# Two transformer blocks on one core: in the even layer, weight loads go ahead of the gate tile, and ScalarE moves two products ahead of two roots

## The chip, the cores and the metric

One core of one Trainium2 chip runs the whole program in one launch. The metric is the device time of one execution in microseconds, lower is better. Engines are named as in the profile: PE is TensorE's matmul, PEld its weight load, DVE is VectorE, ACT is ScalarE, POOL is GpSimd, SP is SyncE, which issues the DMAs.

## The reference, cut to what matters

The program is a chain of layers on a 512 x 1024 float32 activation: an even layer (gated linear recurrence and short convolution), an odd layer (gated linear attention), then a second block with feed-forward and attention layers. Only the even layer is touched:

```python
h = rmsnorm(x, norm_pre)
proj = h @ w_in                      # 1024 -> 6 x 1024
xa, za, xb, gb, gc, zb = split(proj)
ua = centred_dwconv(xa, conv_w, 2) + conv_b
r, i = sigmoid(gates(ua))            # per head 128 x 128, two directions
a = exp(-8 r softplus(-lam)); b = sqrt(-expm1(2 log a)) * (i * ua)
h_f, h_b = scan forward, scan backward
ya = (h_f + h_b) * silu(za)
yb = gb * centred_dwconv(gc * xb, sc_w, 1) * silu(zb)
y = concat(ya, yb) @ w_out
```

## The kernel before, in words

**Tiling.** The activation lies transposed: features on the 128 partitions, 512 tokens along the free axis, so one matrix of 1024 x 128 weights ("slot") gives one tile of 128 x 512 outputs. Every float32 product is made of three fp32r products, `hi*hi`, `hi*lo` and `lo*hi`: `product` (lines 357 to 368) issues 3 x 8 = 24 matmuls per slot (lines 364, 365, 366).

**The even layer** goes through eight channels (heads) 0 to 7. A channel has six slots, numbered n = 0 to 5 within it and s = 0 to 47 over the layer: xa, xb, gc, gb, zb (silu), za (silu). On PE `even_channel` (line 668) runs the six products of a channel into four PSUM banks (s % 4) and then `even_gates` (line 658): eight matmuls (line 664) that multiply the channel's `ua` by the four gate matrices. Channel 0 is special: it works on the input before its norm is known. In channel 1 the gates of channel 0 are put behind its first product; from channel 2 on the order is six products, then the gates of the same channel.

**Weights.** SP loads each slot's 512 KB into a ring of four places (`even_weight`, DMA at line 591). A place may be written when POOL has split the slot before it (semaphore `w_ready`). POOL (`split_slot`, lines 321 to 335) casts a slot to `w_hi` (line 332) and subtracts to get `w_lo` (line 334). These two have two places each, so a slot's split waits until PE has finished the product two slots before (`slots_used`).

**The gate tile.** `gw` has two places (jj = channel % 2). One DMA of 264 KB (`gate_weight`, line 594) brings the gate matrices, their biases and the convolutions' weights of a channel. It may be written when the channel two before is entirely done. That is what SP waits for (`even_channel_done`, line 615), ahead of the gate tile and of all six slots of the channel.

**The order on ACT** (`even_act`, line 1314). Per channel: six moves of products out of PSUM (line 1325; the last two are Silu), four sigmoids of the gates (lines 1337, 1338), two Exp and two Tanh (lines 1346, 1348), and two square roots (line 1355), each of which waits for DVE. The moves free PSUM banks: product s + 4 waits for move s (`even_moved`).

**The order on DVE** (`even_dve`, line 1739). Per channel: the convolution of xa (lines 1774, 1777), which ends in `ua_ready`, for which the gates on PE wait; the convolution of xb (1801 to 1811); then, once ACT has the decays, squares and factors (1817 to 1821), two times product and scan (1825, 1828), the sum (1830) and the product with silu(za) (1832), which signals `even_channel_done`. DVE takes the channels strictly one after the other, so `ua` of a channel stands behind all of the channel before.

After channel 7 PE goes on with the layer's output product (`even_out`, lines 712 to 714), and the rest of the program follows.

Of the kernel before, what the change touches and what calls it, by code (L numbers as in the profile page):

```python
# [10 lines left out]
ACT = mybir.ActivationFunctionType  # L11
# [5 lines left out]
T = 512  # L17
# [13 lines left out]
RING = 4  # L31
# [73 lines left out]
def build(nc, x_in, consts_in, gates_in, weights, out):  # L105
    ctx = ExitStack()
    with ctx:
        sem = {}
# [46 lines left out]
        ps = ctx.enter_context(nc.psum_tensor("ps", [P, 8, 512], F32))  # L155
# [24 lines left out]
        for name, slots, cols in STREAM:  # L180
            first[name] = n0
            n0 += slots
        slots_of = {name: slots for name, slots, _ in STREAM}
        cols_of = {name: cols for name, _, cols in STREAM}

        def used(name, n):

            return n + (first[name] + 2)
# [229 lines left out]
        xa_pad, xb_s, gc_s, gb_s, szb, sza, ua = (r.tiles(2, n) for n in (516, T, T, T, T, T, T))  # L418
# [168 lines left out]
        @block.sync  # L587
        def _(sp):
            def even_weight(i, s):
                cols = cols_of["even_in"]  # L590
                sp.dma_start(ring[:, s % RING, 0:cols], weights["even_in"][12 * i + s]).then_inc(landed[s % RING], 16)

            def gate_weight(i, jj):
                sp.dma_start(gw[:, jj, :], gates_in[2 * i + jj]).then_inc(gate_landed[jj], 16)

            sp.dma_start(consts[:, 0:N_FIRST], consts_in[:, 0:N_FIRST]).then_inc(sem["const_landed"], 16)
            even_weight(0, 0)
            for k in range(DT):
                sp.dma_start(res[:, k, :], x_in[:, k, :]).then_inc(x_landed[k], 16)
                if k == 1:  # L600
                    even_weight(0, 1)
            even_weight(0, 2)
            even_weight(0, 3)
            gate_weight(0, 0)
            gate_weight(0, 1)
            sp.dma_start(consts[:, N_FIRST:N_CONSTS], consts_in[:, N_FIRST:N_CONSTS]).then_inc(sem["consts_landed"], 16)
            for s in range(RING, 12):
                sp.wait_ge(sem["w_ready"], s + 1)
                even_weight(0, s)
            for name, slots, cols in STREAM:  # L610
                if name == "even_in":
                    with sp.Fori(0, RG_HEADS // 2 - 1) as i:
                        for jj in range(2):

                            sp.wait_ge(sem["even_channel_done"], 2 * i + (jj + 3))
                            gate_weight(i + 1, jj)
                            for n in range(6):
                                s = 6 * jj + n
                                sp.wait_ge(sem["w_ready"], 12 * i + (s + 13))
                                even_weight(i + 1, s)  # L620
                    continue
                with sp.Fori(0, slots // RING) as i:
                    for j in range(RING):

                        sp.wait_ge(sem["w_ready"], RING * i + (first[name] + j + 1))
                        sp.dma_start(ring[:, j, 0:cols], weights[name][RING * i + j]).then_inc(landed[j], 16)
            for t in range(DT):
                sp.wait_ge(sem["res_done"], RES["ffn2_1"] + DT + t + 1)
                sp.dma_start(out[:, t, :], res[:, t, :]).then_inc(sem["out_stored"], 16)
            sp.wait_ge(sem["out_stored"], 16 * DT)  # L630
# [667 lines left out]
        def _(act):  # L1298
# [12 lines left out]
            rinv_act(act, "even_pre")  # L1311
            nc.scalar.activation(rinv_even, root[:, :], ACT.Exp, scale=-0.5).then_inc(sem["rinv_copied"], 1)

            def even_act(i, jj, c=None):
                act.wait_ge(sem["even_channel_done"], 2 * i + (jj + 1))

                dsts = [(xa_pad[:, jj, 2:2 + T], ACT.Copy), (xb_s[:, jj, :], ACT.Copy), (gc_s[:, jj, :], ACT.Copy),
                        (gb_s[:, jj, :], ACT.Copy), (szb[:, jj, :], ACT.Silu), (sza[:, jj, :], ACT.Silu)]
                for n, (dst, func) in enumerate(dsts):
                    s = 6 * jj + n  # L1320
                    if c == 0:
                        act.wait_ge(sem["plain_scaled"], n + 1)
                    else:
                        act.wait_ge(sem["slots_used"], 12 * i + used("even_in", s + 1))
                    nc.scalar.activation(dst, ps[:, s % RING, :], func).then_inc(sem["even_moved"], 1)
                    if c == 0 and n == 3:
                        for k in range(DT):
                            act.wait_ge(sem["even_scaled"], k + 1)
                            nc.scalar.activation(hi[:, k, :], even_tmp[k % 2], ACT.Copy).then_inc(sem["even_high"], 1)
                if c == RG_HEADS - 1:  # L1330
                    y_highs(DT, 2 * DT - 1)
                    act.wait_ge(sem["even_channel_done"], 1 + RG_HEADS)
                    y_highs(0, DT - 1)
                par = gw[:, jj, 4 * P:4 * P + 16]
                act.wait_ge(sem["gates_done"], 2 * i + (jj + 1))
                for d in range(2):
                    nc.scalar.activation(rg[d], ps[:, 4 + 2 * d, :], ACT.Sigmoid, bias=par[:, 2 * d:2 * d + 1])
                    a = nc.scalar.activation(ig[:, d, :], ps[:, 5 + 2 * d, :], ACT.Sigmoid,
                                             bias=par[:, 2 * d + 1:2 * d + 2])
                a.then_inc(sem["gates_read"], 1)  # L1340
                act.drain()

                if c == 0:
                    act.wait_ge(sem["nsp_ready"], 1)
                for d in range(2):
                    nc.scalar.activation(ag[:, d, :], rg[d], ACT.Exp, scale=nsp_c[:, jj, d:d + 1])
                for d in range(2):
                    a = nc.scalar.activation(hg[d], rg[d], ACT.Tanh, scale=nsp_c[:, jj, d:d + 1])
                a.then_inc(sem["decay_ready"], 1)
                if c == RG_HEADS - 1:  # L1350
                    act.wait_ge(sem["yb_done"], 1)
                    y_highs(2 * DT - 1, 2 * DT)
                for d in range(2):
                    act.wait_ge(sem["factor_ready"], 4 * i + (2 * jj + d + 1))
                    nc.scalar.activation(rg[d], tg[d], ACT.Sqrt, scale=-1.0).then_inc(sem["root_b_ready"], 1)

            def y_highs(k0, k1):
                for k in range(k0, k1):
                    x_hi = hi[:, k, :] if k < DT else lo[:, k - DT, :]
                    nc.scalar.activation(x_hi, y_even[:, k, :], ACT.Copy).then_inc(sem["y_high"], 1)  # L1360

            for jj in range(2):
                even_act(0, jj, jj)
            with act.Fori(0, RG_HEADS // 2 - 2) as i:
                for jj in range(2):
                    even_act(i + 1, jj)
            for jj in range(2):
                even_act(RG_HEADS // 2 - 1, jj, RG_HEADS - 2 + jj)
# [1012 lines left out]
        def _(pool):  # L2381
# [30 lines left out]
            for j in range(1, 2 * RING):  # L2412
                split_slot(pool, "odd_out", j // RING, j % RING)
            split_first(pool, "ffn1_in_0_0")
            split_pool(pool, *(name for name, _, _ in ffn_stream("ffn1", 0)[1:]), "sb_qk", "sb_v", "sb_late",
                       "sb_out", *(name for name, _, _ in ffn_stream("ffn2", 0)), "kv_c", "kv_kv")
            for n in range(7):
                split_slot(pool, "cmp_w1", n // RING, n % RING)
# [214 lines left out]
```

## Time and profile before

| | us |
|---|---|
| median of 3 runs | 2738.15 (2737.18 to 2739.89) |
| the profiled execution | 2736.76 |
| its span | 2734.9 |
| PE busy | 2696.8 (99%) |
| POOL busy | 1624.7 (59%) |
| DVE busy | 1356.1 (50%) |
| ACT busy | 708.7 (26%) |

The span is from the first to the last instruction; what lies around it is 1.86 us. Columns of a timeline row are start in us, duration in us, engine, line, operation, tiles, shapes, number of instructions merged (x), and in brackets the engine's idle time before it and what released it. Ends of matmuls are modelled, so one matmul's duration is longer than the step to the next.

### The profile page before, as it was taken

What the parts mean: (1) busy time and instruction counts of PE and PEld (TensorE: products, weight loads), DVE (VectorE), ACT (ScalarE), POOL (GpSimd) and SP (SyncE); (2) the same over time, 40 slices, a digit from 0 to 9 for tenths busy, and PEclk for the clock granted to TensorE, in tenths of its full rate; (3) what the DMA queues carried; (4) which work ended last, traced back from release to release, by engine and by line L of the source; (5) the groups of instructions that cost most, each with busy time, mean ns of one, the idle gap of its engine ahead of it and who ended that gap; (6) DMA issues with size and microseconds to landing.
All of it is one profiled execution on the core that took longest, in us unless ns stands there. A gap on an engine that the chain in (4) does not pass through costs nothing.

```text
span 2734.9 us, 36055 instructions
## 1 busy us (share of the span) xinstructions
PE 2696.8 (99%) x13190; PEld 2166.0 (79%) x13190; DVE 1356.1 (50%) x1605; ACT 708.7 (26%) x1235; POOL 1624.7 (59%) x949
## 2 busy tenths in 40 slices
PE   9999999999999999999999999999999999999999
PEld 6777777877888888867888888788888766888887
DVE  7878824574432461176440454642246777543242
ACT  4443423343200110284210113310012476211010
POOL 5666755524665666603665665566666799566565
PEclk9999999999999999999999999999999999999999
DMA  4222222202332322301332332333232100233232
GB/s 180 101 97 91 89 93 86 84 24 75 94 115 77 98 95 93 93 8 47 93 110 83 100 100 92 124 100 113 80 100 92 55 1 2 85 100 115 77 98 87
DMA packets 62028, 235.58 MB, mean 86 GB/s; under 512 B 6880, under 2 KB 7008, under 8 KB 61792
## 3 DMA queue, kind: packets, MB, share of 16 engines
q1 hardware_dynamic: 61920, 234.14, 26.9%
q8 instruction: 68, 1.11, 0.2%
q14 instruction: 40, 0.33, 0.0%
HBM read 232.02 MB, written 2.10 MB: 86 GB/s over the span
## 4 chain that ended last, share of the span: by engine, by line
PE 80%; DVE 6%; POOL 4%; PEld 3%; ACT 2%; issue 2%; DVEq 1%; DMA 1%; PEldq 0%; POOLq 0%; ACTq 0%; SPq 0%
PE ps L364 23%; PE ps L366 23%; PE ps L365 23%; POOL arena L2458 4%; PE ps L388 1%; PE ps L382 1%; PE ps L383 1%; PE ps L1045 1%; PEld ps L712 1%; PEld ps L713 1%; PEld ps L714 1%; PE ps L1029 1%; POOL w_lo L334 0%; DVE w_tails L1828 0%; DMA ring<-in_even_in 0%
## 5 line engine op out<-in xcount | busy, mean ns | idle before, releaser
L334 POOL TENSOR_TENSOR w_lo<-ring,w_hi 128x1024 fp32r<-128x1024 f32 (+2 forms) x382 | 985.9, 2581 | 56.5 <-issue 3.1
L332 POOL CAST w_hi<-ring 128x1024 fp32r<-128x1024 f32 (+2 forms) x382 | 435.1, 1139 | 910.7 <-PE ps L366 724.8
L364 PE MATMUL ps<-hi,w_hi 128*128 128x512 f32 x2064 | 809.0, 392 | 5.3 <-POOL w_lo L334 2.4
L365 PE MATMUL ps<-lo,w_hi 128*128 128x512 f32 x2064 | 803.2, 389 | 0.0
L366 PE MATMUL ps<-hi,w_lo 128*128 128x512 f32 x2064 | 803.2, 389 | 0.0
L364 PEld LDWEIGHTS ps<-hi,w_hi 128*128 128x128 f32 x2064 | 387.4, 188 | 93.1 <-POOL w_lo L334 6.0
L365 PEld LDWEIGHTS ps<-lo,w_hi 128*128 128x128 f32 x2064 | 387.5, 188 | 81.9 <-issue 2.1
L366 PEld LDWEIGHTS ps<-hi,w_lo 128*128 128x128 f32 x2064 | 387.4, 188 | 80.8
L364 PE MATMUL ps<-hid_hi,w_hi 128*128 128x512 f32 x704 | 274.4, 390 | 0.0
L365 PE MATMUL ps<-hid_lo,w_hi 128*128 128x512 f32 x704 | 274.0, 389 | 0.0
L366 PE MATMUL ps<-hid_hi,w_lo 128*128 128x512 f32 x704 | 273.9, 389 | 0.0
L2047 DVE TENSOR_TENSOR hid_lo<-arena,hid_hi 128x512 f32 (+1 forms) x88 | 222.1, 2524 | 80.2 <-ACT hid_hi L1516 80.2
L1514 ACT ACTIVATE ps<-ps 128x512 f32<-128x512 f32 x88 | 51.2, 582 | 629.3 <-DVE ps L2039 629.3
L2063 DVE SCALAR_TENSOR_TENSOR res<-ps,res 128x512 f32<-128x512 f32 x64 | 44.3, 692 | 310.4 <-PE ps L366 310.4
L2044 DVE TENSOR_TENSOR arena<-arena,ps 128x512 f32<-128x512 f32 x88 | 60.5, 687 | 275.4 <-PE ps L366 275.0
L246 DVE SCALAR_TENSOR_TENSOR lo<-res,consts,hi 128x512 fp32r<-128x512 f32 x64 | 150.8, 2365 | 32.0 <-ACT hi L240 31.7
L1516 ACT ACTIVATE hid_hi<-arena 128x512 f32 (+1 forms) x88 | 55.7, 633 | 410.8 <-DVE arena L2044 410.8
L364 PEld LDWEIGHTS ps<-hid_hi,w_hi 128*128 128x128 f32 x704 | 132.1, 188 | 28.6 <-POOL w_lo L334 1.3
L365 PEld LDWEIGHTS ps<-hid_lo,w_hi 128*128 128x128 f32 x704 | 132.1, 188 | 27.5
L366 PEld LDWEIGHTS ps<-hid_hi,w_lo 128*128 128x128 f32 x704 | 132.1, 188 | 27.4
L2458 POOL TENSOR_SCALAR arena<-arena 128x512 f32<-128x512 f32 (+3 forms) x124 | 132.9, 1092 | 15.2 <-DVE arena L2334 15.1
L2039 DVE TENSOR_TENSOR ps<-ps,rinv 128x512 f32<-128x512 f32 x88 | 61.5, 699 | 117.8 <-PE ps L366 107.8
(367 smaller groups left out, 3318.8 us busy)
## 6 DMA issues: line engine op xcount, KB each, us to landing
ring<-in_ffn_in SPq DMA_DIRECT2D x176, 512.0 KB, 3.6
ring<-in_even_in SPq DMA_DIRECT2D x48, 512.0 KB, 4.9
ring<-in_ffn_out SPq DMA_DIRECT2D x32, 768.0 KB, 4.3
ring<-in_ffn_out SPq DMA_DIRECT2D x32, 640.0 KB, 3.9
ring<-in_even_out SPq DMA_DIRECT2D x16, 512.0 KB, 3.6
ring<-in_sb_qk SPq DMA_DIRECT2D x12, 512.0 KB, 3.6
ring<-in_odd_v SPq DMA_DIRECT2D x8, 512.0 KB, 3.6
ring<-in_odd_r SPq DMA_DIRECT2D x8, 512.0 KB, 3.7
```

What stands on the lines that cost most here:

```text
L246: nc.vector.scalar_tensor_tensor(lo[:, t, :], res[:, t, :], con("g_" + f)[:, t:t + 1], hi[:, t, :].bitcast(F32), ALU.mult, ALU.subtract).t ...
L332: nc.gpsimd.tensor_copy(high[:, j % 2, 0:cols], ring[:, j, 0:cols])
L334: nc.gpsimd.tensor_tensor(low[:, j % 2, 0:cols], ring[:, j, 0:cols], high[:, j % 2, 0:cols].bitcast(F32), ALU.subtract).then_inc(sem["w_re ...
L364: nc.tensor.matmul(bank, w_hi[:, j % 2, w], x_hi[:, k, :], start=(k == 0), stop=False)
L365: nc.tensor.matmul(bank, w_hi[:, j % 2, w], x_lo[:, k, :], start=False, stop=False)
L366: mm = nc.tensor.matmul(bank, w_lo[:, j % 2, w], x_hi[:, k, :], start=False, stop=(k == kt - 1))
L1514: nc.scalar.activation(gate, gate, ACT.Silu).then_inc(sem["silu_done"], 1)
L1516: nc.scalar.activation(hid_hi[:, 2 * i + j, :], wide[:, j, :], ACT.Copy)\
L2039: V.tensor_tensor(gate, gate, rinv[:, :], ALU.mult).then_inc(sem["gate_scaled"], 1)
L2044: V.tensor_tensor(wide[:, j, :], wide[:, j, :], up, ALU.mult).then_inc(sem["hidden_wide"], 1)
L2047: V.tensor_tensor(hid_lo[:, 2 * i + j, :], wide[:, j, :], hid_hi[:, 2 * i + j, :].bitcast(F32), ALU.subtract)\
L2458: op = G.tensor_scalar(part, part, coef[:, s % 4, i, e:e + 1], None, ALU.mult)
```

## The change

On SP the wait for the channel two before and the load of the gate tile move from ahead of a channel's slot n = 0 to ahead of its slot n = 4. Slots 0 to 3 of a channel then wait only for their places in the ring. This holds for channels 2 to 7; the loads of channels 0 and 1 are unchanged.

On ACT the body of the move loop becomes a function `even_move`. The moves of channel 1's slots n = 0 and n = 1 are issued within channel 0, behind its Tanh and ahead of its two square roots; in channel 1 the loop starts at n = 2. No instruction is added or removed on any engine.

```diff
                     with sp.Fori(0, RG_HEADS // 2 - 1) as i:
                         for jj in range(2):
 
-                            sp.wait_ge(sem["even_channel_done"], 2 * i + (jj + 3))
-                            gate_weight(i + 1, jj)
                             for n in range(6):
                                 s = 6 * jj + n
+                                if n == RING:
+                                    sp.wait_ge(sem["even_channel_done"], 2 * i + (jj + 3))
+                                    gate_weight(i + 1, jj)
                                 sp.wait_ge(sem["w_ready"], 12 * i + (s + 13))
                                 even_weight(i + 1, s)
```

```diff
+            def even_move(i, jj, n, c=None):
+                dst, func = [(xa_pad[:, jj, 2:2 + T], ACT.Copy), (xb_s[:, jj, :], ACT.Copy), (gc_s[:, jj, :], ACT.Copy),
+                             (gb_s[:, jj, :], ACT.Copy), (szb[:, jj, :], ACT.Silu), (sza[:, jj, :], ACT.Silu)][n]
+                s = 6 * jj + n
+                if c == 0:
+                    act.wait_ge(sem["plain_scaled"], n + 1)
+                else:
+                    act.wait_ge(sem["slots_used"], 12 * i + used("even_in", s + 1))
+                nc.scalar.activation(dst, ps[:, s % RING, :], func).then_inc(sem["even_moved"], 1)
+
             def even_act(i, jj, c=None):
                 act.wait_ge(sem["even_channel_done"], 2 * i + (jj + 1))
 
...
-                for n, (dst, func) in enumerate(dsts):
...
+                for n in range(2 if c == 1 else 0, 6):
+                    even_move(i, jj, n, c)
                     if c == 0 and n == 3:
                         for k in range(DT):
                             act.wait_ge(sem["even_scaled"], k + 1)
...
                 for d in range(2):
                     a = nc.scalar.activation(hg[d], rg[d], ACT.Tanh, scale=nsp_c[:, jj, d:d + 1])
                 a.then_inc(sem["decay_ready"], 1)
+                if c == 0:
+                    even_move(0, 1, 0)
+                    even_move(0, 1, 1)
                 if c == RG_HEADS - 1:
```

## Rows read from the trace of the kernel before

**Rows 1.** The page, part 1: busy time, share of the span, instructions.
```profile
PE 2696.8 (99%) x13190; PEld 2166.0 (79%) x13190; DVE 1356.1 (50%) x1605; ACT 708.7 (26%) x1235; POOL 1624.7 (59%) x949
```

**Rows 2.** Waits of PE, 40 to 300 us: total us, times, longest us.
```profile
PE ps L364 <- POOL w_lo L334: 2.4, 4, 1.9
PE ps L364 <- ACT arena L1325: 1.3, 1, 1.3
```

**Rows 3.** Timeline of PE: gates of channels 1, 2, 3, 6, 7; restarts.
```profile
72.96 0.50 PE L364 MATMUL ps<-hi,w_hi 128*128 128x512 f32 x1 [1.28 <-ACT arena L1325]
...
83.98 3.60 PE L664 MATMUL ps<-arena 128*128 128x512 f32 x8
...
89.47 0.50 PE L364 MATMUL ps<-hi,w_hi 128*128 128x512 f32 x1 [1.90 <-POOL w_lo L334]
...
122.24 3.59 PE L664 MATMUL ps<-arena 128*128 128x512 f32 x8
...
158.36 3.60 PE L664 MATMUL ps<-arena 128*128 128x512 f32 x8
...
268.10 3.59 PE L664 MATMUL ps<-arena 128*128 128x512 f32 x8
...
304.19 3.60 PE L664 MATMUL ps<-arena 128*128 128x512 f32 x8
```

**Rows 4.** Waits of SP's DMA queue, 40 to 300 us.
```profile
SPq L594 <- DVE arena L1832: 139.4, 6, 30.0
```

**Rows 5.** Timeline of ACT: channel 0's roots, and moves of slots.
```profile
61.73 1.28 ACT L1355 ACT_TABLE_LOAD   x1
66.77 0.63 ACT L1355 ACTIVATE ring<-w_tails 128x512 f32<-128x512 f32 x1 [3.77 <-DVE w_tails L1819]
...
78.73 0.60 ACT L1325 ACTIVATE arena<-ps 128x512 f32<-128x512 f32 x1 [3.06 <-PE ps L366]
...
106.12 0.60 ACT L1325 ACTIVATE arena<-ps 128x512 f32<-128x512 f32 x1 [4.18 <-PE ps L366]
...
153.12 0.60 ACT L1325 ACTIVATE arena<-ps 128x512 f32<-128x512 f32 x1 [3.54 <-PE ps L366]
...
298.94 0.60 ACT L1325 ACTIVATE arena<-ps 128x512 f32<-128x512 f32 x1 [3.54 <-PE ps L366]
```

**Rows 6.** Timeline of POOL: casts and one subtraction of the split.
```profile
85.22 1.44 POOL L332 CAST w_hi<-ring 128x1024 fp32r<-128x1024 f32 x1 [9.16 <-DMA ring<-in_even_in]
...
106.25 1.15 POOL L332 CAST w_hi<-ring 128x1024 fp32r<-128x1024 f32 x1 [1.60 <-PE ps L366]
...
111.69 1.19 POOL L332 CAST w_hi<-ring 128x1024 fp32r<-128x1024 f32 x1 [1.02 <-PE ps L366]
113.03 2.58 POOL L334 TENSOR_TENSOR w_lo<-ring,w_hi 128x1024 fp32r<-128x1024 f32 x1
...
299.11 1.50 POOL L332 CAST w_hi<-ring 128x1024 fp32r<-128x1024 f32 x1
```

**Rows 7.** Timeline of DVE: ends of channels, convolutions of xa.
```profile
77.22 0.69 DVE L1825 TENSOR_TENSOR w_tails<-arena,ring 128x512 f32<-128x512 f32 x1
...
81.36 2.42 DVE L1777 SCALAR_TENSOR_TENSOR arena<-arena 128x512 f32<-128x512 f32 x3
...
105.81 0.69 DVE L1825 TENSOR_TENSOR w_tails<-arena,ring 128x512 f32<-128x512 f32 x1
...
113.44 4.39 DVE L1777 SCALAR_TENSOR_TENSOR arena<-arena 128x512 f32<-128x512 f32 x3
...
152.99 2.41 DVE L1777 SCALAR_TENSOR_TENSOR arena<-arena 128x512 f32<-128x512 f32 x3
...
298.86 5.09 DVE L1777 SCALAR_TENSOR_TENSOR arena<-arena 128x512 f32<-128x512 f32 x3
```

**Rows 8.** Windows of line 638 (26 equal matmuls): us, PE busy (count), PEld, PEclk.
```profile
1.37:5.37 4.00, 4.00 (x13) 1.96 (x14) 1.00 0.86 261
5.37:7.95 2.58, 2.57 (x15) 1.23 (x12) 1.00 0.87 294
```

More of the change, by code:

```diff
@@ L1312, in _ @@
             nc.scalar.activation(rinv_even, root[:, :], ACT.Exp, scale=-0.5).then_inc(sem["rinv_copied"], 1)
+            def even_move(i, jj, n, c=None):
[7 more added lines that the diff above has]
+                nc.scalar.activation(dst, ps[:, s % RING, :], func).then_inc(sem["even_moved"], 1)
             def even_act(i, jj, c=None):
                 act.wait_ge(sem["even_channel_done"], 2 * i + (jj + 1))
-                dsts = [(xa_pad[:, jj, 2:2 + T], ACT.Copy), (xb_s[:, jj, :], ACT.Copy), (gc_s[:, jj, :], ACT.Copy),
-                        (gb_s[:, jj, :], ACT.Copy), (szb[:, jj, :], ACT.Silu), (sza[:, jj, :], ACT.Silu)]
-                for n, (dst, func) in enumerate(dsts):
[L1320 to L1325, printed above, removed]
+                for n in range(2 if c == 1 else 0, 6):
+                    even_move(i, jj, n, c)
                     if c == 0 and n == 3:
```

## The prediction

> **What bounds the kernel now.** I read the page first: PE is busy 99% of the span [rows 1], so only time in which PE stands still can be won or lost. The waits of PE over the even layer give what there is: 1.3 us for a move by ACT and 2.4 us in four waits for POOL's `w_lo` [rows 2]. The timeline of PE says where they are and what they really cost. I write G(c) for the start of the gates of channel c: G(1) 83.98, G(2) 122.24, G(3) 158.36, G(6) 268.10, G(7) 304.19 [rows 3].
>
> An undisturbed channel takes 36.12 us (G(2) to G(3)) or 36.09 (G(6) to G(7)). From this:
> - Stall A, at 72.96, ahead of channel 1's slot n = 4: 1.28 idle, and the first matmul takes 0.50 where the step is 0.23, so 1.55 us. Its bank is freed by ACT's move of channel 1's slot n = 0, which stands behind channel 0's roots.
> - Stall B, at 89.47, behind the gates of channel 1: G(1) to G(2) is 38.26, so 38.26 - 36.12 = 2.14 us. POOL had idled 9.16 us for the weights [rows 6], because SP sat on the wait for channel 0.
> - Stall C, three small waits behind the gates of channels 3, 4 and 5: G(3) to G(6) is 109.74, less 3 x 36.11 = 1.41 us.
>
> Together 5.1 us or 0.19% of the time. All three are what the change addresses. About 0.2% (5.5 us) is what a measurement of this kernel can tell from no change.
>
> **SP's part.** SP waits 139.4 us in six waits for `even_channel_done` [rows 4]. Slots n = 0 to 3 no longer stand behind it. Moved behind them is one DMA of 264 KB per channel; its reader on DVE comes a whole channel later, so I cost it at nothing, and the cover is about 30 us of the channel between. Slots 4 and 5 stay behind the wait and are needed by POOL four products later: nothing. The splits of a channel's slots 0 and 1 then start when PE has finished the second product before, and no longer when the DMA lands. B and C go: -2.14 and -1.41.
>
> **ACT's part.** The two copies come right behind Tanh, where ACT loads a table at 61.73 and then idles 3.77 us until 66.77 [rows 5]. Both products are finished by then (A is on ACT's side, not on PE's). Two copies at the 0.60 of a move fit in the 3.77, so the roots are not late: cost nothing; if the cover were gone it would be 1.2 us on DVE's chain. A goes: the gates of channel 1 could start at 83.98 - 1.55 = 82.43.
>
> **What is late next.** Those gates need `ua` of channel 1. DVE makes it with three instructions that start at 81.36 and take 2.42, ready at 83.78 [rows 7], 0.20 ahead of the gates. So even with DVE unchanged, of A's 1.55 only 0.2 us would be kept.
>
> And DVE does not stay unchanged. In the kernel before, POOL idled for 9.16 us up to 85.22 [rows 6], and that is just where DVE finished channel 0 and made `ua` of channel 1. With the loads ahead, POOL splits channel 2's slot 0 as soon as channel 1's n = 4 is finished. Before, ACT's move of it started at 78.73 [rows 5]; less 1.55 it is 77.18, and POOL's cast comes 0.13 behind such a move (106.12 and 106.25) [rows 5, 6]: 77.31. The next cast follows one product later, at 82.6.
>
> The trace has this very case one channel later. The cast of 106.25 meets the end of channel 1 on DVE (line 1825 at 105.81, 0.44 ahead of the cast; at channel 0 it is 77.22, 0.09 ahead), the next cast of 111.69 and its subtraction from 113.03 to 115.61 meet the convolution, and DVE's three instructions take 4.39 instead of 2.42 and end at 117.83 [rows 6, 7]. From the first cast to `ua` ready: 117.83 - 106.25 = 11.58 us. Put on 77.31, `ua` of channel 1 is ready at 88.89. PE would stand from 82.43 to 88.9: 6.5 us, a new stall.
>
> Bounds for it: with nothing of POOL in DVE's way `ua` is ready at 83.78; with all of 11.58 at 88.89. I take the upper value, because all that makes it (same lines, same order, casts 5.4 us apart) is the same. The row shows how it comes about: the three would take 2.42, POOL's subtraction ends at 115.61, and they end 2.22 behind that, as if the first had been held until it was over.
>
> Sum at channel 1: G(1) goes from 83.98 to 88.9, +4.9; B is gone, -2.14; so PE enters channel 2 2.8 us later than before. C gives back 1.41 until channel 6, if `ua` of the later channels is in time. There POOL's cast will come 0.13 behind the move of n = 4. Before, at 152.99, DVE was undisturbed and 2.96 ahead of the gates (152.99 + 2.41 = 155.40 against 158.36) [rows 3, 7]. The case with POOL at work stands in channel 7, where the next slots were never behind that wait: move at 298.94, cast at 299.11, DVE's three from 298.86 to 303.95, gates at 304.19 [rows 3, 5 to 7]. They are in time by 0.24, and the channel took 36.09. So C is given back: -1.41. Sum so far: +1.4 us.
>
> **The restart of PE.** The trace has no idle time of PE of over 1.90 us, and behind that one PE is back at full pace after one matmul [rows 3]. The one place where PE starts from rest is the kernel's start: 26 equal matmuls, 13 of them counted in the first 4.00 us and 15 in the next 2.58 [rows 8]; those across an edge are counted twice, so 12 and 14, a step of 0.33 and then 0.18. The granted clock reads 1.00 (2.4 GHz) in both, but the pace of the first is that of 1.2 GHz. Bounds of a restart after 6.5 us: nothing (the pause of 1.90), or all eight gate matmuls at half pace, 3.6 us more. Between them lies the price of that start, 12 x (0.33 - 0.18) = 1.8 us. I take it: 6.5 us is over three times the longest pause that left the pace alone.
>
> Total +1.4 + 1.8 = +3.2 us. On the profiled execution, 2736.76 (span 2734.9 and 1.86 around it), that makes 2740.0. The median is 1.4 above it, 2738.15: 2741.3.
>
> **The rivals.**
> 1. *PE restarts at full pace.* For: the pause of 1.90. Against: the kernel's start. Then +1.4: 2739.5. The Trainium skill (TensorE: Matmul & The Clock Gate, the part on the mystery of the warm-up) calls the throttled state the default, which activity releases; by it this rival would fall and the restart would be at the lower clock. No row here shows a pause of such a length.
> 2. *DVE is held less.* POOL's and DVE's instructions could fall so that only one subtraction lies in the way, or none. Then `ua` is ready at 83.78 to 86.5. At 83.78: G(1) 83.9, -0.1 - 2.14 - 1.41 = -3.65: 2734.5. At 86.5: +2.5 - 2.14 - 1.41 = -1.05: 2737.1. Against: the row at 113.44.
> 3. *Slower beyond doubt: `ua` is late in every later channel.* The place is DVE's line 1777 in channels 2 to 6. It decides whether the first of the three is issued ahead of POOL's cast. From the rows it starts at 152.99 with the move at 153.12, so the cast is due at 153.25: 0.26 us. If POOL comes first, it goes as at 111.69, where `ua` is ready 6.14 behind the cast, 6.27 behind the move. The gates come 5.24 behind it (153.12 to 158.36). Five channels x 1.03 = 5.1 us: 2746.4. Against: channel 7, where it was in time. The Trainium skill (SBUF — State Buffer, "Who interferes with whom") lets the one that issues first hold the shared ports for its whole instruction; by it the order at that one place decides, for either price.
> 4. *The change doesn't do what it says*, or C's return is eaten by a wait of the same size: the copies wait longer than I think, or a slot of the ring is late. Between 2738.2 and 2742.7.
>
> **How the numbers follow.** Chances: forecast 0.48 (2741.3, its own range 2740 to 2743.2), rival 1 0.20 (2739.5), rival 2 0.11 (2734.5 to 2737.1), rival 3 0.13 (2746.4), rival 4 0.08. The forecast, rival 1, rival 4 and the upper edge of rival 2 lie in 2737.0 to 2744.5; left out are rival 3 and most of rival 2. Faster by over 0.2% means under 2732.7: only beyond rival 2, 0.04. Slower by over 0.2% means over 2743.6: rival 3 and 0.05 from the forecast with a long half-paced stretch, 0.18. Within 0.2%: 0.78.
>
> **What would show it.** In the profile after: no stall of PE ahead of slot n = 4 of channel 1; POOL's idle time of 9.16 us gone, a cast near 77.3; the end of line 1777 in channel 1 near 88.9 and PE idle some 6.5 us ahead of the gates there, released by DVE's line 1777; no wait for `w_lo` behind gates; G(3) to G(6) 108.3; matmuls of line 664 in channel 1 stretched from 3.6 us to 5 or more. The prediction is wrong at its main step if `ua` of channel 1 is ready ahead of 86 us, wrong at the restart if the gates take 3.6, and wrong at C if line 1777 ends behind the due time of the gates in channels 3 to 6.

## The result, and the profile after

The changed kernel takes 2741.73 us (median of 22 runs), the kernel before, timed between them, 2738.28 us (median of 22). The ratio is 1.0014, 95% interval 1.0008 to 1.002: slower by 3.45 us. The direction is clear of noise; the size is below the 0.2% that I had set as the bound of "no change", and the upper end of the interval lies on that bound. The forecast was 2741.3.

The profiled execution took 2744.0 us, its span is 2742.2. Lines of code below the ACT function have moved by seven in the changed kernel: line 1777 is now 1784, 1832 is 1839, the gates' 664 is 665, the moves' 1325 is 1323.

The waits of PE from 40 to 300 us, where there were two kinds and five waits before [rows 2]:

```profile
PE ps L665 <- DVE arena L1784: 6.5, 1, 6.5
```

One wait is left, the one that the change made. The waits of SP's queue in the same stretch [rows 4]:

```profile
SPq L591 <- POOL w_lo L334: 209.0, 38, 17.9
...
SPq L594 <- DVE arena L1839: 6.7, 1, 6.7
```

The loads no longer wait for the end of a channel (139.4 us in six waits before, 6.7 us in one now), but for a free place in the ring. SP's part does what it says.

The timeline of PE, gates of channels 1 to 3, 6 and 7 [rows 3]:

```profile
90.46 6.67 PE L665 MATMUL ps<-arena 128*128 128x512 f32 x8 [6.51 <-DVE arena L1784]
...
129.66 3.59 PE L665 MATMUL ps<-arena 128*128 128x512 f32 x8
...
165.78 3.60 PE L665 MATMUL ps<-arena 128*128 128x512 f32 x8
...
274.11 3.59 PE L665 MATMUL ps<-arena 128*128 128x512 f32 x8
...
310.24 3.60 PE L665 MATMUL ps<-arena 128*128 128x512 f32 x8
```

The stall ahead of slot n = 4 of channel 1 is gone, as is that behind its gates. In their place PE idles 6.51 us ahead of the gates of channel 1, and the gates then take 6.67 instead of 3.60. From G(2) to G(7) it is 180.58, before 181.95: five channels of 36.12 each, and stall C is gone. In channel 2 DVE starts the three instructions of `ua` just ahead of POOL's cast:

```profile
124.20 5.00 DVE L1784 SCALAR_TENSOR_TENSOR arena<-arena 128x512 f32<-128x512 f32 x3
```

```profile
124.55 1.30 POOL L332 CAST w_hi<-ring 128x1024 fp32r<-128x1024 f32 x1 [1.51 <-PE ps L366]
```

The timelines of POOL and DVE at the end of channel 0 [rows 6, 7] show where the 6.51 come from:

```profile
78.69 1.37 POOL L332 CAST w_hi<-ring 128x1024 fp32r<-128x1024 f32 x1 [1.38 <-PE ps L366]
80.19 3.12 POOL L334 TENSOR_TENSOR w_lo<-ring,w_hi 128x1024 fp32r<-128x1024 f32 x1
84.12 1.41 POOL L332 CAST w_hi<-ring 128x1024 fp32r<-128x1024 f32 x1 [0.81 <-PE ps L366]
85.67 2.52 POOL L334 TENSOR_TENSOR w_lo<-ring,w_hi 128x1024 fp32r<-128x1024 f32 x1
```

```profile
78.46 0.69 DVE L1832 TENSOR_TENSOR w_tails<-arena,ring 128x512 f32<-128x512 f32 x1
79.23 1.90 DVE L1835 TENSOR_TENSOR_SCAN w_tails<-arena,w_tails 128x512 f32<-128x512 f32 x1
81.20 2.66 DVE L1837 TENSOR_TENSOR w_tails<-w_tails 128x512 f32<-128x512 f32 x1
83.94 0.69 DVE L1839 TENSOR_TENSOR arena<-w_tails,arena 128x512 f32<-128x512 f32 x1
84.55 1.00 DVE L1776 COPY arena<-arena 128x2 f32<-128x2 f32 x1
...
86.08 4.32 DVE L1784 SCALAR_TENSOR_TENSOR arena<-arena 128x512 f32<-128x512 f32 x3
```

Slot 12 is channel 2's n = 0, slot 13 its n = 1. Slot 12's subtraction, 80.19 to 83.31, holds up the sum at 81.20 (2.66 instead of 0.69); slot 13's, 85.67 to 88.19, holds up the first of the three of `ua` (4.32 for the three instead of 2.42). The two casts cost DVE a little as well: beside them the scan at 79.23 takes 1.90 instead of the 1.22 that it takes in the kernel before (77.99), and the small copy at 84.55 takes 1.00 instead of 0.16. From the cast at 78.69 to `ua` ready at 90.40 it is 11.71 us; the prediction took 11.58 from one channel later. The place in the trace is 1.4 to 1.5 us later than forecast because this execution lost 1.4 us at its start: the gates of channel 0 stand at 53.11, in the execution before at 51.72.

The clock in that pause, windows of the changed kernel (us, busy time and count of PE, PEld, DVE, ACT, POOL; then PEclk, DMA share, GB/s):

```profile
86.00:88.00 2.00, 0.00 (x0) 0.00 (x0) 1.92 (x1) 0.00 (x0) 2.00 (x1) 0.56 1.00 317
...
92.00:94.00 2.00, 2.00 (x3) 0.67 (x2) 1.85 (x3) 0.00 (x0) 0.00 (x0) 0.50 0.00 0
...
96.00:98.00 2.00, 2.00 (x7) 1.12 (x7) 0.00 (x0) 0.83 (x2) 0.00 (x0) 0.88 0.00 0
```

The granted clock falls to 0.50 (1.2 GHz) while PE stands still, stays there through the gates, and comes back only behind 96 us (a mean of 0.88 from 96 to 98).

The ledger of the two profiled executions: +1.39 at the start, +5.09 from G(0) to G(1) (32.26 to 37.35), +0.94 from G(1) to G(2) (-2.14 for stall B, +3.07 for the slow gates), -1.37 from G(2) to G(7): 6.05 us. I don't count the first as the change's, nor a further 1.2 us in the odd layer. A stretch of 8 us there has a granted clock of 0.79, and the interval around it takes 17.1 us instead of 15.9; one of the other kernels' profiles (the one with channel 2's loads late, below) has the same dip and the same 17.1. What is left as the change's own cost in the profile is 5.09 + 0.94 - 1.37 = 4.66 us.

### The profile page after: what moved, and what is told of

It reads as the page before. It is cut to its first block, busy times and chain, and to the rows that moved or that the text cites. A ratio compares the mean times of both kernels' runs of the same rounds, so it can differ in the third digit from the quotient of the medians.

```text
span 2742.2 us, 36055 instructions
## 1 busy us (share of the span) xinstructions
PE 2700.8 (98%) x13190; PEld 2169.7 (79%) x13190; DVE 1357.2 (49%) x1605; ACT 709.0 (26%) x1235; POOL 1624.9 (59%) x949
## 4 chain that ended last, share of the span: by engine, by line
PE 83%; DVE 5%; POOL 4%; PEld 3%; ACT 2%; issue 1%; DVEq 1%; PEldq 0%; POOLq 0%; ACTq 0%; DMA 0%
PE ps L364 24%; PE ps L366 23%; PE ps L365 23%; POOL arena L2465 4%; PE ps L388 1%; PE ps L382 1%; PE ps L383 1%; PE ps L1046 1%; PE ps L665 1%; PEld ps L713 1%; PEld ps L714 1%; PEld ps L715 1%; PE ps L1030 1%; DVE arena L2307 0%; PE ps L813 0%
## 5 line engine op out<-in xcount | busy, mean ns | idle before, releaser
L246 DVE SCALAR_TENSOR_TENSOR lo<-res,consts,hi 128x512 fp32r<-128x512 f32 x64 | 139.8, 2193 | 31.9 <-ACT hi L240 31.7
```

The source lines that it names most:

```text
L246: nc.vector.scalar_tensor_tensor(lo[:, t, :], res[:, t, :], con("g_" + f)[:, t:t + 1], hi[:, t, :].bitcast(F32), ALU.mult, ALU.subtract).t ...
```

## The experiments

The theory: POOL's splits of slots 12 and 13 hold DVE up, `ua` of channel 1 is late, PE pauses, and the pause costs the clock as well. The rivals: ACT's reordering is what makes `ua` late; the slow gates have another cause; the early splits hurt every channel. Every kernel was timed in 5 rounds against the kernel before (medians of 11 runs; the kernel before 2737.98 to 2738.77 in the three sets).

**One part alone.** First SP's part, with ACT's function as in the kernel before (only the first diff of the change):

> SP's part alone (ACT as before). Theory (POOL's splits of slots 12 and 13 hold DVE, ua of channel 1 is late, PE pauses and restarts at half pace): stall A of 1.5 us stays, and the pause ahead of the gates of channel 1 is 6.5 us all the same, because it hangs on POOL's cast, which is tied to the product of slot 10; gates near 6.7 us. In all 1.5 us worse than the changed kernel, +5 us against the kernel before. Rival (ACT's copies ahead of the roots are what makes ua late): pause under 1 us, gates 3.6, -3.5 us against before.

Measured: 2742.01 against 2738.34, ratio 1.0016 [1.0007, 1.0025]. Its timeline of PE:

```profile
74.31 0.50 PE L364 MATMUL ps<-hi,w_hi 128*128 128x512 f32 x1 [1.28 <-ACT arena L1326]
...
90.34 6.05 PE L665 MATMUL ps<-arena 128*128 128x512 f32 x8 [4.86 <-DVE arena L1778]
```

And POOL's cast of slot 12 and DVE's three:

```profile
80.22 1.17 POOL L332 CAST w_hi<-ring 128x1024 fp32r<-128x1024 f32 x1 [2.81 <-PE ps L366]
```

```profile
85.35 4.94 DVE L1778 SCALAR_TENSOR_TENSOR arena<-arena 128x512 f32<-128x512 f32 x3
```

Stall A stays, and the pause is there without ACT's part, so the rival falls. But I was wrong by its size (4.86, not 6.5) and so by the time (+3.7, not +5). The gates of channel 1 start at 90.34, where they start at 90.46 in the whole change. The cast of slot 12 is 1.53 later (80.22), and so catches DVE later; `ua` is ready at 90.29, 10.07 us behind it, not 11.7. Whatever ACT's part wins ahead of the pause, the pause takes: +3.7 us without it, +3.45 with it, which these measurements can't tell apart.

Then ACT's part alone, with SP's order as before (only the second diff):

> ACT's part alone (SP as before). Theory: stall A is gone, PE waits some 1.3 us for ua ahead of the gates of channel 1 in its place, ua is ready as before within 0.3 us, stall B shrinks by nothing, since the first matmul behind the gates still hangs on the load: 0 +- 0.5 us against before. Rival (the copies delay the roots and with them ua): ua 1.2 us or more later, and a pause of 3 us or more.

Measured: 2738.59 against 2738.34, ratio 1.0003 [0.9994, 1.0012]. Its timeline of PE:

```profile
85.23 3.70 PE L664 MATMUL ps<-arena 128*128 128x512 f32 x8 [1.12 <-DVE arena L1783]
90.88 0.50 PE L364 MATMUL ps<-hi,w_hi 128*128 128x512 f32 x1 [1.94 <-POOL w_lo L334]
```

The pause ahead of the gates is 1.12 (DVE), behind them 1.94 (POOL's `w_lo`), as forecast. ACT's part is worth nothing that can be measured alone. In this profile, with SP's old order, only one of the three small waits of stall C is there: G(2) to G(7) is 181.02, where the profile of the kernel before has 181.95 and the changed one 180.58. So C is worth 0.4 us in one execution and 1.4 in another.

**Is it POOL's work at that moment?** The change, with one wait more on POOL:

```diff
+            for n in range(RING, 4 * RING):
+                if n == 3 * RING:
+                    pool.wait_ge(sem["ua_ready"], 2)
+                split_slot(pool, "even_in", n // RING, n % RING)
-            with pool.Fori(0, slots_of["even_in"] // RING - 1) as i:
+            with pool.Fori(0, slots_of["even_in"] // RING - 4) as i:
                 for j in range(RING):
-                    split_slot(pool, "even_in", i + 1, j)
+                    split_slot(pool, "even_in", i + 4, j)
```

> The change, and POOL waits for ua of channel 1 ahead of its split of slot 12. Theory: DVE runs undisturbed, ua is ready about 11.4 - 5 = 6.4 us behind the due time of the cast instead of 11.6; PE pauses 1.4 us ahead of the gates, not 6.5, the gates take 3.6; a small wait for w_lo (under 1 us) comes behind them. -2 to -3 us against before. Rival (ua is late for another reason than POOL's work): the pause stays over 5 us and w_lo comes late on top, +6 us or more.

Measured: 2734.34 against 2738.34, ratio 0.9985 [0.9976, 0.9994], 7.5 us better than the change by the differences to the kernel before, and 1 us more than I expected. Its waits of PE, 40 to 300 us, and DVE in the place:

```profile
PE ps L665 <- DVE arena L1784: 1.1, 1, 1.1
PE ps L364 <- POOL w_lo L334: 0.3, 1, 0.3
```

```profile
81.01 0.69 DVE L1837 TENSOR_TENSOR w_tails<-w_tails 128x512 f32<-128x512 f32 x1
...
83.09 2.42 DVE L1784 SCALAR_TENSOR_TENSOR arena<-arena 128x512 f32<-128x512 f32 x3
```

With POOL still, the sum takes 0.69 and the three 2.42; the pause is 1.1. This shows the cause: POOL's early splits make `ua` late. The same wait ahead of slot 13 instead (`n == 3 * RING + 1`) parts the two splits:

> The change, and POOL waits for ua of channel 1 ahead of its split of slot 13 alone; slot 12 is split early. Theory: slot 12's split costs DVE 2.0 to 2.7 us at the end of channel 0, slot 13's the other 3 us in the convolution; ua of channel 1 is ready 8.5 to 9 us behind the cast of slot 12 (11.6 in the change), PE pauses 3.3 to 3.9 us; with a pause that long the gates take over 4.5 us. -1 to +1 us against before. Rival (only slot 13's split matters): pause 1.2 us, -3.5 us.

Measured: 2739.28 against 2737.98, ratio 1.0006 [0.9997, 1.0015].

```profile
79.17 1.35 POOL L332 CAST w_hi<-ring 128x1024 fp32r<-128x1024 f32 x1 [1.40 <-issue]
80.67 3.12 POOL L334 TENSOR_TENSOR w_lo<-ring,w_hi 128x1024 fp32r<-128x1024 f32 x1
```

```profile
81.68 2.66 DVE L1837 TENSOR_TENSOR w_tails<-w_tails 128x512 f32<-128x512 f32 x1
...
85.72 2.41 DVE L1784 SCALAR_TENSOR_TENSOR arena<-arena 128x512 f32<-128x512 f32 x3
```

And the gates of channel 1 on PE:

```profile
88.18 5.40 PE L665 MATMUL ps<-arena 128*128 128x512 f32 x8 [3.73 <-DVE arena L1784]
```

`ua` is ready 88.13 - 79.17 = 8.96 us behind the cast, the pause is 3.73, and the gates take 5.40. So of the 6.5 us pause, slot 12's split, cast and subtraction, makes 2.6 (3.73 - 1.12), slot 13's 2.8 (6.51 - 3.73), and 1.1 would be there with neither. The time is a little above my range.

**The clock.** The change, and PE kept at work while it waits:

```diff
+                if c == 1:
+                    pe.wait_ge(sem["gates_read"], 2)
+                    for n in range(36):
+                        nc.tensor.matmul(ps[:, 7, 0:3 * P], ident_1, masks[:, 0:3 * P], start=True, stop=True)
                 pe.wait_ge(sem["ua_ready"], 2 * i + (jj + 1))
```

> The change, and 36 matmuls of 128 x 384 on a bank of no use, ahead of the wait for ua in channel 1, so that PE does not stand still. Theory (the clock falls in the pause): the gates of channel 1 take 3.6 us instead of 6.7, granted clock 1.00 throughout; 2 to 3 us better than the changed kernel, +0.5 to +1.5 against before. Rival (the gates are slow for another reason, such as DVE or DMA at work beside them): gates stay near 6.7, no gain or a loss.

Measured: 2739.65 against 2738.34, ratio 1.0006 [0.9997, 1.0015], +1.3 us where the change has +3.45. Its timeline of PE and one window:

```profile
82.16 6.02 PE L664 MATMUL ps<-masks 128*128 128x384 bf16 x36
...
88.98 3.70 PE L669 MATMUL ps<-arena 128*128 128x512 f32 x8 [0.80 <-DVE arena L1788]
```

```profile
86.00:92.00 6.00, 5.21 (x21) 2.52 (x20) 5.54 (x8) 0.00 (x0) 0.71 (x1) 1.00 0.44 143
```

`ua` is as late as ever, and nothing is computed sooner, yet the gates take 3.70 at a granted clock of 1.00. The slow gates were the clock's, worth 2.1 us by the medians and 3.0 in the two profiles. The slowest of these 11 runs (2740.33) is below the fastest of the changed kernel's 22 (2740.87).

**Does it hurt in every channel?** The change, but for channel 2 SP's wait and gate tile stand ahead of slot n = 0 again; channels 3 to 7 as in the change:

```diff
+                    channel(0, 0, 0)
+                    channel(0, 1, RING)
+                    with sp.Fori(0, RG_HEADS // 2 - 2) as i:
+                        for jj in range(2):
+                            channel(i + 1, jj, RING)
```

> The change, but channel 2's loads wait for channel 0 ahead of all its slots, as before; channels 3 to 7 as in the change. Theory: stall A turns into a wait for ua of 1.1 us, stall B stays near 1.9 us, no w_lo waits in channels 3 to 5: -1 to -1.6 us against before. Rival (the early splits hurt in each channel, not in channel 1 alone): pauses ahead of later gates, +1 us or more.

Measured: 2737.05 against 2738.77, ratio 0.9996 [0.9987, 1.0005]: -1.7 us, with both waits back in channel 1 and no other:

```profile
85.46 3.70 PE L669 MATMUL ps<-arena 128*128 128x512 f32 x8 [1.26 <-DVE arena L1788]
90.43 0.50 PE L364 MATMUL ps<-hi,w_hi 128*128 128x512 f32 x1 [1.26 <-POOL w_lo L334]
```

The interval holds 1, so the gain is not shown by the times alone. The two waits of channel 1 are 1.26 us each, and no gates of a later channel are waited for, so the rival's pauses are not there. In the profile G(2) to G(7) is 180.58 (123.20 to 303.78), as in the changed kernel. By the profile the early loads are right for channels 3 to 7 and wrong at channel 2 only.

**Is ACT's part worth anything once `ua` is early?** SP's part with POOL's wait ahead of slot 12, ACT as before:

> SP's part alone, and POOL waits for ua of channel 1 ahead of its split of slot 12; ACT as before. Theory (ACT's part is worth only the 0.2 us by which ua was ahead of the gates): as the run with the change and the same wait, within 0.5 us: -3.5 to -4 us against before. Rival (ACT's part is worth stall A's 1.5 us): -2.3 us.

Measured: 2735.35 against 2738.77, ratio 0.9988 [0.9979, 0.9997], -3.4 us, a little less than the -3.5 to -4 expected, where the run with both has -4.0. In the profiles G(0) to G(2) is 68.96 with ACT's old order and 68.72 with the new: the difference of 0.24 us is all that ACT's part brings, about the 0.2 by which `ua` was ahead of the gates. The medians differ by 0.6, within their noise.

**Two attempts at all 5.1 us.** The first makes `ua` of channel 1 earlier instead of holding POOL:

```diff
+                if c == 0:
+                    dve.wait_ge(gate_landed[1], 16)
+                    V.tensor_copy(nsp_c[:, 1, :], nsp2[:, 1, :])
+                    convolve(1)
                 for d in range(2):
                     dve.drain()
                     dve.wait_ge(sem["root_b_ready"], 4 * i + (2 * jj + d + 1))
...
+                if c == 1:
+                    act.wait_ge(sem["even_channel_done"], 3)
                 act.wait_ge(sem["gates_done"], 2 * i + (jj + 1))
```

> The change, and DVE makes ua of channel 1 within channel 0, behind its factors and ahead of its two scans; ACT's sigmoids of channel 1 wait for the end of channel 0. Theory: no pause ahead of the gates of channel 1, gates 3.6 us, no wait for w_lo behind them, G(1) to G(2) 36.1 us; all of the three stalls, 5.1 us, are won: -4.5 to -5.5 us against before. Rival (DVE has no time left: what is put ahead comes back as a late ua of channel 2 or late gates_read, since channel 0 ends 3 us or more later): a pause of 1 to 3 us ahead of the gates of channel 2, and -2 to -3 us.

Measured: 2739.06 against 2738.77, ratio 1.0002 [0.9993, 1.0011]. Its timeline of PE and the windows of the place:

```profile
83.70 3.59 PE L665 MATMUL ps<-arena 128*128 128x512 f32 x8
...
122.42 5.39 PE L665 MATMUL ps<-arena 128*128 128x512 f32 x8 [2.45 <-DVE arena L1788]
```

```profile
122.00:124.00 2.00, 1.58 (x4) 0.86 (x5) 2.00 (x2) 0.00 (x0) 2.00 (x1) 0.95 0.10 41
124.00:126.00 2.00, 2.00 (x4) 0.83 (x3) 1.85 (x3) 0.00 (x0) 0.49 (x1) 0.50 0.18 12
```

The rival was right by its mechanism, and too hopeful by its -2 to -3 us. In the profile G(0) to G(7) is 0.7 us shorter than in the kernel before, and that with 1.8 us lost to the slow gates; the medians show no gain at all. The gates of channel 1 are on time, channel 0 ends on DVE at 90.49 instead of 84.63 in the change, and the stall comes out one channel later: 2.45 us, and the clock falls again (5.39). DVE, with POOL's splits beside it, had no time left: moving its work alone won nothing, where keeping POOL off it did. Both together were not tried.

The second is the kernel with POOL's wait ahead of slot 12, and 15 matmuls of no use (4, 2 and 9) ahead of three waits in PE's first product. In most of the profiles, though not in that of the kernel before, the gates of channel 0 start at 53.0 to 53.6 us and the clock dips around 15 us.

> The change, POOL's wait ahead of slot 12, and 15 matmuls of no use in three waits of PE in its first 14 us. Theory (in most executions the clock falls once in those first 25 us, the first product then takes 1.5 us more): gates of channel 0 start near 51.5 us and not 53.1 or later, granted clock 1.00 from 10 to 22 us; -5 to -5.5 us against before. Rival (the start is bound by the loads): gates of channel 0 stay at 53, -4 us.

Measured: 2733.53 against 2737.98, ratio 0.9983 [0.9974, 0.9992], the fastest of all, 4.45 us faster than the kernel before, and short of the 5 to 5.5 that I expected. Gates of channel 0 at 51.66, a granted clock of 1.00 from 10 to 22 us. The step against the run without the fill is small on the median (-4.45 against -4.0, within the intervals); its runs spread over 1.5 us, those of that kernel over 3.0. That the fill prevents the dip is not shown by one profile: two without it, the kernel before and the run with PE kept at work in channel 1, have no dip there either.

## Why the prediction was right

The direction and the mechanism came as forecast, and so did the time: 3.2 us were named, 3.45 measured. That the two numbers are so close is in part luck. The profile puts the change's own cost at 4.66, 1.5 above the forecast, of which 1.3 are the restart of PE; the medians show 1.2 less than the profile, and no run says why. Point by point:

- *A, B and C go.* Right: none of the five old waits is left.
- *`ua` is late next, by POOL's work.* Right, and shown by holding POOL. The pause was named at 6.5 and is 6.51, and without the 1.39 of the start the cast comes at 77.30, forecast 77.31; the step that carried it, reading the same sequence one channel later instead of adding up durations, gave 11.58 for 11.71. What I had not seen is that this figure is no constant: with the cast 1.53 later it was 10.07.
- *Of A only 0.2 us could be kept.* Right as a bound: 0.24 once POOL is held, nothing measurable otherwise.
- *C is given back, with `ua` in time by 0.24.* Right: in channel 2 of the changed kernel the three end at 129.20 and the gates start at 129.66. G(3) to G(6) is 108.33, forecast 108.3. Rival 3 did not happen: in all of channels 2 to 6 the first of DVE's three is issued ahead of the cast, by 0.25 to 0.35 us (124.20 and 124.55 in channel 2). The Trainium skill's rule for the ports shared by the two (SBUF — State Buffer, "Who interferes with whom"), that the first to issue holds them, agrees with the order on both sides of the trace: beside the scan issued at 79.23 POOL's subtraction takes 3.12 instead of 2.66, and that subtraction makes DVE's sum take 2.66 instead of 0.69. By length only the second is near a full hold: the subtraction starts 0.94 ahead of the scan's end and takes 0.46 longer.
- *The restart at half pace, 1.8 us.* The mechanism is right, the term was mis-sized: the gates took 6.67, 3.07 more in the profile, and filling the pause won back 2.1 us by the medians. The price that I took from the kernel's start was low: here nearly all of the gates ran at half pace, close to the upper bound of 3.6. The rule of the Trainium skill (TensorE: Matmul & The Clock Gate, the part on the mystery of the warm-up), that the throttled state is the default which activity releases, agrees: 0.50 in the pause and behind it.

The profiled execution, 2744.0, is 4 us above the 2740.0 that the working gives: 1.3 us are the restart, 1.4 the start of the program and 1.2 the odd layer, both of them dips of the clock that the profile of the kernel before, from which the working starts, does not have. The first of them stands in eight of the eleven profiles, so the 1.4 by which the median was put above that profile may be it; that is not shown.

## What to carry to other kernels

When a load is moved ahead, ask what its landing sets going and beside whom: here it let POOL split weights just where DVE, which POOL holds up, was on the critical path. Hold the new work until the critical piece is through; one wait turned +3.45 us into -4.0. A pause of PE of 2.45 us and more cost the clock on top in these runs, so price a pause with its restart.

## What the runs showed of the hardware that I had not expected

Short pauses cost the clock too. Behind 1.90, 1.94, 1.26, 1.12 and 0.80 us the gates or products went on at full pace, behind 2.45 us the gates took 5.39, behind 3.73 us 5.40, behind 4.86 us 6.05 and behind 6.51 us 6.67, where 3.59 is full pace. At the kernel's start the clock dipped in eight of the eleven profiled executions (a mean of 0.58 to 0.90 between 10 and 16 us; 1.00 in the kernel before, in the run with PE kept at work in channel 1, whose start is as in the change, and in the run with the start filled), and the gates of channel 0 then start at 53.0 to 53.6 us, not at 51.5 to 51.7. The kernel before and the changed one have the same wait in front of it, 1.81 and 1.82 us, and only the second dipped behind it: the same pause goes with a loss of some 1.4 us in one execution and with nothing in another. In the run with POOL's wait ahead of slot 12 the clock is already down before that wait (0.74 from 10 to 12 us), so the wait is not the whole of it. What decides was not tried.
